# Two-block transformer, one core: early query weights, late bias rows, block-wise convolution taps

## The reference

```python
h = rmsnorm(x, norm1_g)
z = h @ w_in + b_in
glu_val, glu_gate, q, k, v, g_conv, g_attn = jnp.split(z, ...)
conv_out = conformer_conv(glu_val, glu_gate, ...)   # u = val * sigmoid(gate), 31 causal taps per channel,
                                                    # layer norm, silu, product with w_conv_out
attn_out = swa_sink_attention(rope(q), rope(k), v, sinks) @ w_attn_o
merged = sigmoid(g_conv) * conv_out + sigmoid(g_attn) * attn_out
x = x + merged @ w_out
h2 = rmsnorm(x, norm2_g)
q = (h2 @ w_peer_q).reshape(B, S, 8, 2, 128)        # 8 query heads; 16 best of 128 x 128 experts for each
a = gelu(u_emb[idx] . h2);  x = x + sum(gate * a * v_emb[idx])
```

## Time and profile before

| | us |
|---|---|
| median of 3 executions (lowest, highest) | 1623.15 (1622.27, 1624.31) |
| the profiled execution | 1624.08 |
| its span in the trace | 1622.2 |
| PE busy | 1448.3 (89%) |
| DVE busy | 989.6 (61%) |
| ACT busy | 621.2 (38%) |
| POOL busy | 317.8 (20%) |

### The profile page before, as it was taken

The page is one execution under the profiler, slowest core; times in us unless marked ns, Lnnn a source line. Parts: engine busy times, 40 slices in busy tenths (PEclk is TensorE's granted clock), DMA queues, the critical chain, the costliest instruction groups (busy, mean ns, idle before and its releaser), DMA issues.

```text
span 1622.2 us, 16485 instructions
## 1 busy us (share of the span) xinstructions
PE 1448.3 (89%) x5922; PEld 992.2 (61%) x5922; DVE 989.6 (61%) x1967; ACT 621.2 (38%) x1293; POOL 317.8 (20%) x298
## 2 busy tenths in 40 slices
PE   7999999989987777787988769989999999999998
PEld 5868897644542222333333227867888879778886
DVE  3996776667766767776676453236555455565553
ACT  1014572233333333533333224454444335644442
POOL 2000000334534444434435410400000000000000
PEclk9999999999999999999999989999999999999999
DMA  8345653999999999999999964422545443255451
GB/s 318 130 156 149 126 187 119 422 419 415 414 421 420 420 420 420 415 389 417 410 413 419 420 260 157 152 97 104 207 161 202 147 190 142 86 202 187 176 197 62
DMA packets 51777, 428.55 MB, mean 264 GB/s; under 512 B 6648, under 2 KB 6792, under 8 KB 9584
## 3 DMA queue, kind: packets, MB, share of 16 engines
q0 software_dynamic: 40464, 279.18, 43.1%
q1 hardware_dynamic: 11232, 148.33, 24.1%
HBM read 422.49 MB, written 4.98 MB: 264 GB/s over the span
## 4 chain that ended last, share of the span: by engine, by line
PE 65%; DMA 20%; DVE 8%; ACT 4%; issue 2%; POOL 1%; SPq 0%; DVEq 0%; ACTq 0%; POOLq 0%
DMA pool<-uv,experts 19%; PE psum L741 17%; PE psum L1112 11%; PE psum L871 11%; PE psum L872 10%; PE psum L873 10%; PE psum L774 3%; DVE pool L2037 2%; PE psum L818 2%; DMA ring<-stream 1%; DVE ring_lo L1692 1%; ACT diag L1528 1%; ACT xn L1204 1%; POOL pool L699 1%; ACT coef L1522 1%
## 5 line engine op out<-in xcount | busy, mean ns | idle before, releaser
L1112 PE MATMUL psum<-pool,diag 128*128 128x512 f32 x1024 | 477.0, 615 | 119.9 <-ACT diag L1528 119.8
L2037 DVE CUSTOM_DVE_ANT_0 pool<-pool,xn 128x1024 f32<-128x1024 f32 x256 | 313.3, 1225 | 201.0 <-DMA pool<-uv,experts 199.0
L1112 PEld LDWEIGHTS psum<-pool,diag 128*128 128x128 f32 x1024 | 191.8, 194 | 396.2 <-issue 205.6
L699 POOL DMA_INDIRECT pool<-uv,experts x256 | 286.5, 1119 | 505.3 <-PE psum L1112 357.6
L1692 DVE TENSOR_TENSOR ring_lo<-ring,w_hi 128x2048 fp32r<-128x2048 f32 x76 | 173.9, 2292 | 114.0 <-ACT w_hi L1296 114.0
L741 PE MATMUL psum<-hT,ring 128*128 128x256 f32 (+1 forms) x832 | 175.0, 371 | 5.9 <-DMA ring<-stream 4.1
L1518 ACT ACTIVATE acts<-dots 128x2 f32<-128x2 f32 x128 | 26.0, 203 | 379.5 <-DVE dots L2037 379.4
L1296 ACT ACTIVATE w_hi<-ring 128x2048 fp32r<-128x2048 f32 x76 | 144.4, 1908 | 65.5 <-PE psum L873 37.7
L741 PEld LDWEIGHTS psum<-hT,ring 128*128 128x128 f32 x832 | 151.7, 196 | 28.6 <-issue 8.2
L871 PE MATMUL psum<-w_hi,h_hi 128*128 128x512 f32 x400 | 161.3, 403 | 5.1 <-DVE h_lo L1731 4.2
L872 PE MATMUL psum<-ring_lo,h_hi 128*128 128x512 f32 x400 | 157.5, 394 | 0.0
(11 more groups left out here) (267 smaller groups left out, 1858.4 us busy)
## 6 DMA issues: line engine op xcount, KB each, us to landing
ring<-stream SPq DMA_DIRECT2D x66, 2048.0 KB, 7.7
pool<-uv,experts POOLq DMA_INDIRECT x256, 12.7
ring<-stream SPq DMA_DIRECT2D x3, 1024.0 KB, 4.8
t_scratch<-tab POOLq DMA_DIRECT2D x1, 2048.0 KB, 56.8
rpb_scratch<-tab POOLq DMA_DIRECT2D x1, 1792.0 KB, 22.9
ring<-stream SPq DMA_DIRECT2D x1, 1792.0 KB, 6.9
row<-rows POOLq DMA_DIRECT2D x1, 1672.0 KB, 15.5
ring<-stream SPq DMA_DIRECT2D x1, 1664.0 KB, 6.5
```

The lines of the kernel that those rows point to most:

```text
L699: gp.indirect_dma_start(out=gath[:, n % NROWS, :], out_offset=None, in_=uv, in_offset=bass.IndirectOffsetOnAxis(ap=experts[:, n:n + 1], ax ...
L1112: last = nc.tensor.matmul(psum[:, RB + half, :], diag[:, n % NDIAG, :], gath[:, n % NROWS, D + 512 * half:D + 512 * half + 512], start=k = ...
L2037: ins = V.tensor_tensor_reduce(out=row_u, in0=row_u, in1=xn[:, n // SLOTS, :], scale=1.0, scalar=0.0, op0=ALU.mult, op1=ALU.add, accum_out ...
```

## The change

1. The chunk pq 2 (query heads 4 and 5) leaves the stream. It comes as an input of its own, in four DMAs of 512 KB, which SP issues right behind wout 0, into four places that are idle until the expert stage is over: `k1z`, the last 1024 columns of `att`, part of the table buffer, and the first 1024 columns of `row`. SP waits for attno's last product and for two stores to HBM before them. `query` reads the weights of heads 4 and 5 from there.
2. `row` and `keys` are issued by POOL behind the `rpb` pieces and after the second GLU bank is filled.
3. A GLU chunk's columns are ordered so that each bank holds values and gates of one block. ACT and DVE work by blocks (8 steps, not 4), the sigmoid's table is loaded ahead, and the taps are dealt out as 13, 15 x 6 and 84, then 12, then 4 to a head; two open blocks alternate.
4. PE does 12 products of constants with 256 columns into the bank of the next transposes before it waits for the second tile of `mix0`, and 6 before it waits in `first_pair` of the second layer. Their results are overwritten.

```diff
+EARLY_QUERY = 2
...
-    out += [(("pq", i), 4096) for i in range(4)]
+    out += [(("pq", i), 4096) for i in range(4) if i != EARLY_QUERY]
...
-TAPS_AFTER_GLU = (28, 31, 31, 80)
+TAPS_AFTER_GLU = (13, 15, 15, 15, 15, 15, 15, 84)
 TAPS_AFTER_ROPE = 12
-TAPS_IN_HEAD = 5
+TAPS_IN_HEAD = 4
...
+WARM_MIX_NORM, WARM_PAIR = 12, 6
...
-        glu_sig = view(pool, 13296, 2, 512)
+        glu_sig = view(pool, 13296, KD, S)
...
+        query_pieces = [v.rearrange("p (k n) -> p k n", k=2) for v in (
+            k1z[:, :, :, :].rearrange("p n c s -> p (n c s)"), att[:, 6144:7168], spare[:, 2048:3072], row[:, 0:1024])]
...
                 sp.dma_start(ring[:, n % NSLOT, 0:width], src).then_inc(chunk_landed[n % NSLOT], 16)
+                if name == ("wout", 0):
+                    sp.wait_ge(bank_filled, FILL_NO["attno", 1, 1] + 1)
+                    sp.wait_ge(t5_stored, 16)
+                    sp.wait_ge(rpb_stored, 16)
+                    for c, piece in enumerate(query_pieces):
+                        sp.dma_start(piece, early_query[:, 1024 * c:1024 * c + 1024].rearrange("p (k n) -> p k n", k=2)
+                                     ).then_inc(early_query_landed, 16)
...
-            gp.dma_start(row[:, :], rows.to_broadcast([P, NROW])).then_inc(row_landed, 16)
-            gp.dma_start(keys.rearrange("p m n -> p (m n)"), keys_in).then_inc(keys_landed, 16)
...
             gp.wait_ge(rpb_landed, 16 * HEADS2)
+            gp.wait_ge(bank_filled, FILL_NO["glu", 0, 1] + 1)
+            gp.dma_start(row[:, :], rows.to_broadcast([P, NROW])).then_inc(row_landed, 16)
+            gp.dma_start(keys.rearrange("p m n -> p (m n)"), keys_in).then_inc(keys_landed, 16)
...
+            def begin_warm(name, count):
+                dst = begin(name)
+                for _ in range(count):
+                    nc.tensor.matmul(dst[:, 0:S], ident, cst[:, 0:S], start=True, stop=True)
+                return dst
...
+            def tile_transposes(name, t, src, warm=0):
+                first = begin_warm((name, t, 0), warm) if warm else None
                 pe.wait_ge(xn_ready, xn_before[name] + t + 1)
...
+                dst = begin_warm(first + (0,), WARM_PAIR) if layer == 1 and q == 0 else begin(first + (0,))
                 pe.wait_ge(h_split, split_before + 2)
-                tile_products(first, layer, q, halves, 0)
+                tile_products(first, layer, q, halves, 0, dst)
...
+                    if head // 2 == EARLY_QUERY:
+                        pe.wait_ge(early_query_landed, 16 * len(query_pieces))
+                        w = [query_pieces[k // 2][:, k % 2, :] for k in range(KD)]
...
-            tile_transposes("mix0", 1, xn[:, 1, :])
+            tile_transposes("mix0", 1, xn[:, 1, :], WARM_MIX_NORM)
...
+            nc.scalar.activation(unused, eps, ACT.Sigmoid)
+            for m in range(KD):
+                b = wait_filled(act, ("glu", m // 2, m % 2))
+                nc.scalar.activation(glu_sig[:, m, :], b[:, S:2 * S], ACT.Sigmoid, bias=par_("b_glu")[:, KD + m:KD + m + 1]
+                                     ).then_inc(sigmoid_ready, 1)
...
+                    open_blocks = [m for m in range(block_ready[0]) if taps_done[m] < TAPS][:2]
+                    if not open_blocks:
+                        return
+                    turn_taken[0] += 1
+                    m = open_blocks[turn_taken[0] % len(open_blocks)]
...
+            for m in range(KD):
+                dve.wait_ge(sigmoid_ready, m + 1)
+                name = ("glu", m // 2, m % 2)
+                b = wait_filled(dve, name)
+                V.scalar_tensor_tensor(u[:, m, TAPS - 1:], b[:, 0:S], par_("b_glu")[:, m:m + 1], glu_sig[:, m, :],
+                                       ALU.add, ALU.mult).then_inc(emptied_sem(name), 1)
+                wait_emptied(dve, name)
+                block_ready[0] = m + 1
+                conv_taps(TAPS_AFTER_GLU[m])
```

More of the change, by code:

```diff
@@ L768, in token_major_chunks, with transposes @@
                     token_major(name, i, w, act, KD, n)
-            def transposes(name, sources, rows_out=P):
-                dst = begin(name)
+            def transposes(name, sources, rows_out=P, dst=None):
+                if dst is None:
+                    dst = begin(name)
                 for j, src in enumerate(sources):
@@ L775, in transposes @@
                 last.then_inc(bank_filled, 1)
-            def tile_transposes(name, t, src):
+            def tile_transposes(name, t, src, warm=0):
+                first = begin_warm((name, t, 0), warm) if warm else None
                 pe.wait_ge(xn_ready, xn_before[name] + t + 1)
                 for hf in range(2):
-                    transposes((name, t, hf), [src[:, P * k:P * k + P] for k in range(4 * hf, 4 * hf + 4)])
+                    transposes((name, t, hf), [src[:, P * k:P * k + P] for k in range(4 * hf, 4 * hf + 4)],
+                               dst=None if hf else first)
             def wait_tile(name, t):
@@ L900, in half_products, with tile_products @@
                     last.then_inc(part_read, 1)
-            def tile_products(name, layer, q, halves, t):
-                dst = begin(name + (t,))
+            def tile_products(name, layer, q, halves, t, dst=None):
+                if dst is None:
+                    dst = begin(name + (t,))
                 half_products(layer, q, halves, dst, t)
@@ L1846, in _ @@
             V.tensor_tensor(t5vec, t5vec, b[0:HEADS2, :], ALU.add).then_inc(emptied_sem(("t5",)), 1)
-            taps_done = [0]
+            taps_done, tap_step, block_ready = [0] * KD, [0] * KD, [0]
+            turn_taken = [0]
             def conv_taps(count):
[L1852 to L1855, removed]
-                    src, tap = u[:, m, w:w + S], conv_w[:, m, w:w + 1]
[L1857 to L1862, removed]
-                    else:
-                        after(steps[0] - 1)
-                        mark(V.scalar_tensor_tensor(y[:, m, :], src, tap, y[:, m, :], ALU.mult, ALU.add))
@@ L1867, in _ @@
[L1867 to L1871, removed]
-                    ins = V.scalar_tensor_tensor(u[:, m, TAPS - 1:], b[:, S * j:S * j + S], par_("b_glu")[:, m:m + 1],
-                                                 glu_sig[:, i % 2, S * j:S * j + S], ALU.add, ALU.mult)
-                ins.then_inc(emptied_sem(("glu", i, 0)), 1)
-                wait_emptied(dve, ("glu", i, 0))
-                conv_taps(TAPS_AFTER_GLU[i])
+                for _ in range(count):
+                    open_blocks = [m for m in range(block_ready[0]) if taps_done[m] < TAPS][:2]
[3 more added lines that the diff above has]
+                    m = open_blocks[turn_taken[0] % len(open_blocks)]
+                    w = taps_done[m]
+                    taps_done[m] += 1
+                    src, tap = u[:, m, w:w + S], conv_w[:, m, w:w + 1]
+                    if w:
+                        after(tap_step[m])
+                        ins = V.scalar_tensor_tensor(y[:, m, :], src, tap, y[:, m, :], ALU.mult, ALU.add)
+                    else:
+                        ins = V.tensor_scalar(y[:, m, :], src, tap, par_("conv_b")[:, m:m + 1], ALU.mult, ALU.add)
+                    if w == TAPS - 1:
+                        ins.then_inc(conv_ready, 1)
+                    else:
+                        tap_step[m] = mark(ins)
```

28 lines of the change are left out of this document (12 added, 16 removed).

## The result

| | before | changed |
|---|---|---|
| median, us (lowest to highest, executions) | 1623.73 (1622.27 to 1627.02, 4) | 1612.51 (1610.89 to 1613.48, 4) |
| ratio, 95% interval | | 0.9922 (0.9907 to 0.9938) |
| profiled execution, its span | 1624.08, 1622.2 | 1610.89, 1609.1 |
| PE busy, DVE busy | 1448.3, 989.6 | 1452.7, 992.1 |
| measured again, twice, each time beside the kernel before | 1625.01 and 1625.2 | 1611.99 and 1611.03 |

The change gains 0.8 to 0.9%, 11 to 14 us by the three medians. The profiled executions differ by 13.2 us, against 12.7 forecast. The forecast median was 1610.5 us and the measured one is 1612.51.

The account below looks back on a forecast made before the run. PE bounds the kernel after the first chunk's transfer, except the expert stage, bound by DMA bytes. 4.1 + 1.0 - 0.1 + 5.0 + 2.7 = 12.7 us off 1624.08 gives 1611.4, as a median 1610.5; range 1606.5 to 1617.

Parts of the forecast that it names:

- start, transfer: Kernel start: without `row` and `keys` in the flow, the first weight chunk lands earlier and PE starts at 13.10; gain 4.1 us.
- start, clock: PE's first products: fewer run at 1.2 GHz; two readings gave gains of 1.7 and 0.4 us, 1.0 taken, ends 0 and 2.4.
- GLU and taps: GLU banks and DVE's taps: counts unchanged, DVE keeps up with PE; gain 0.
- pieces behind wout 0: SP's queue: four early query-weight pieces delay wout 1 by 1.3 us; cost 0.1 us, ends 0 and 1.3.
- expert stage: Expert stage, bound by bytes: one load of 2.10 MB fewer; gain 5.0 us, ends 0 and 5.3.
- behind the last expert: PE's idle 6.30 us before the second tile's transposes: 12 products keep full clock; gain 2.7 us, ends 0 and 3.1.
- first pair: Second layer's first pair: 6 products in a 2.80 us idle piece already at full clock; gain 0, at worst 0.3 lost.
- Rival 2: Start and behind the last expert: clock doesn't follow, slow parts stay; price 1.0 + 2.7, so 1614.2 us; chance 0.14.

Follow-up runs that it names:

- the third execution: The changed kernel unaltered, run a third time beside the kernels with more added products: 1611.03 us, ratio 0.9912 to the kernel before.
- the second one: The changed kernel unaltered, run a second time beside the kernel before: 1611.99 us, ratio 0.9917.

## Why the prediction was right

The direction, the size and the order of the terms held. By the prediction's steps, measured on the profiled pair and on the experiment that undoes the step (by medians; for the pieces' cost and the first pair, by the profile):

| step | forecast | profiled pair | undone alone |
|---|---|---|---|
| start, transfer | 4.1 | 3.8 | 5.5, with the clock |
| start, clock | 1.0 (0 to 2.4) | 1.1; 2.8, outside the ends, in another execution | |
| GLU and taps | 0 | 0 | 0 |
| pieces behind wout 0 | -0.1 (-1.3 to 0) | 0.2 | 0 |
| expert stage | 5.0 (0 to 5.3) | 5.0 | 4.4 |
| behind the last expert | 2.7 (0 to 3.1) | 2.7 | 2.8 |
| first pair | 0 | 0 | 0.1 |
| sum | 12.7 | 12.8 of 13.2 | 12.8 |

The terms undone one at a time sum to 12.8 us, and the ratio 0.9922 of 1623.73 is 12.7 us. They lie in different stages, one behind the other on the chain, so they don't share a wait. That the sums agree to 0.1 us is luck: the three medians of the whole gave 11.2, 13.0 and 14.2 us, and each median of a kernel with one step undone is uncertain by 2 to 3 us.

**The start.** The argument by bytes gave 12 to 13 us for the landing; it was 13.3, 3.8 us earlier. The step said that PE would be busy until 13.10 and become the bound. It failed by a little: the small product ran at full clock and PE was free at 12.22, so the chunk stayed the bound. In the third execution the small product took 1.87 us again, and PE waited only 0.18 us for the chunk. The price of the clock was set between two readings, and its upper end of 2.4 was too low: in the kernel before, stretches of 1 us show 3 or 4 records up to 23 us, not only up to 22, and its 448 records took 2.8 us longer than the shortest. The Trainium skill (TensorE: Matmul & The Clock Gate, "What's actually happening") says that the number of slow products at a kernel's start differs between executions. The traces agree. Of ten profiled executions with the late loads and no products added at the start, five took 110.58 us for the 448 records and five 111.95 to 112.27.

**The pieces.** The sum let them run behind wout 0 at 0.418 MB/us and pushed wout 1 by 1.3 us. What the profile shows is 386 GB/s from 222 to 232 us, a little less, and a landing of the last piece 13.5 us after wout 0's issue (220.38 to 233.9), where the sum had 12.7. It doesn't matter, for wout 1, issued at 231.78, landed as long after its issue as before (240.74 - 231.78 = 8.96, against 246.03 - 236.82 = 9.21). The overlap of 2 us fell into a time in which a lone load hardly moves data: in the kernel before, the two stretches of 1 us from 237 show 197 and 115 GB/s, the next ones 377 to 475. In other executions the copy came sooner, 7.3 us after wout 1's issue in the second one; that one is to be compared with the kernel without pieces (18.73 and 18.82 us from wout 0's issue), and there is no cost in it either. The Trainium skill (DMA: Bandwidth & Descriptors, "Measured") gives 341 GB/s for 1 MB, for transfers issued from GpSimd; the estimate of 1.3 us of cost was worked out from it. The measurement shows no such cost. Here SP issued the transfers, and four were under way together; which of the two makes the difference isn't shown.

**The expert stage** lost the 5.0 us of one load's bytes in the profiled pair. Over twelve profiled executions with the pieces, the stage took 676.7 to 680.9 us from the first gather to the last norm step, 678.2 in the mean, and in both without them 681.7: 0.8 to 5.0 us gained, 3.5 in the mean. The forecast stood at the upper end of what an execution gives, and the 5.0 of the profiled pair is luck in part. The mechanism holds: with all four query chunks in the stream the stage was as long as before in spite of everything else that had changed.

**Behind the last expert** all held: transposes 1.09 us (forecast 1.03), 20.84 us of products, clock 1.00. It is not certain in each execution. Of ten with the 12 products and the idle 1.12 us behind them, seven had 20.84 us and three 22.47 to 22.53, a loss of 1.6 to 1.7 of the 2.7 us. Rival 2 is thus true for a part of the executions. With the 20 products, which leave no idle time ahead of the transposes, the one execution had 20.84.

**Open.** Why the stage of the experts differs in length between executions of the same kernel (676.70, 679.26 and 676.98 us in three) isn't settled. Nor is it why the clock falls or stays behind the same two idle pieces. That `row` and `keys` delay the chunk by the share of the DMA engines that they take fits the bytes and the full engines, but no run separates it from another effect of issuing them early. The last 0.3 us between the last step on DVE (12.82 earlier) and the span (13.1) were not followed.

## What to carry to other kernels

Ask first which transfer the first product waits for, and move behind it each large load that is read much later: 2.8 MB, issued at 30 us and first read at 105 or later, cost nothing and brought 5 us. Where a stage is bound by bytes, its loads can go ahead into memory that is idle earlier, if their queue has a gap in which they are as good as through when the next urgent load may be issued. The gap is the whole matter: an urgent load issued 3.6 us later, with 2.1 MB more ahead of it, cost 6.9 to 7.8 us. Products that are to keep the clock have to last here until just before the awaited rows: a third of the number brought nothing, and 20 instead of 12 gave back 2.1 of the 3.1 us that 12 had gained.

## What the hardware did that was not expected

- The granted clock's column can show 1.00 while the products run at the 1.2 GHz level. In the kernel with the GLU of before, the first stretches touch 4 or 5 records in 1 us, where 6 or 7 are full speed:

```profile
14.00:15.00 1.00, 1.00 (x4) 1.00 0.97 410
15.00:16.00 1.00, 1.00 (x4) 1.00 0.97 411
16.00:17.00 1.00, 1.00 (x5) 1.00 1.13 476
17.00:18.00 1.00, 1.00 (x7) 1.00 0.93 393
```

  In the changed kernel's first profile as many were slow, and there the column fell. The record counts are the surer sign.
- With the late loads, the loss at the start has two forms with about one price, 1.4 to 1.7 us (five of ten executions have neither). In three executions the small product takes 1.87 us and the record counts reach full speed near 16 to 17; in two it takes 1.02 and the granted clock is 0.50 from 14.4 to 17.8.
- Twelve products whose results nobody reads fill an idle piece, but where pieces of 1.12 and 0.99 us are left behind them, the clock can still fall (22.47 us against 20.84, with the same idle times, in three of ten executions).
- Four loads of 512 KB queued together behind one of 2 MB landed 8.3 to 10.9 us after their issue and held up nothing that was waited for.
